# Router logits and token rows made from centred rows instead of normalised ones, in the last LayerNorm before the experts

## Chip, cores and metric

The kernel runs on one core of one Trainium2 chip. The metric is the device time of one execution in microseconds (us); the number quoted is the median of several executions.

## What is computed

One inference step of a two-layer trunk, for 304 tokens at once (16 learned meta tokens, 256 prompt tokens, 8 x 4 sample tokens), width 1024. Layer 0 is a convolution mixer and a dense SwiGLU, layer 1 is latent attention and an expert SwiGLU. The part that is changed is the norm after the attention, and what is made from its result:

```python
xp = layer_norm(ALPHA * xp + mp, ln_g[i, 0], ln_b[i, 0])        # (x - mu) * rsqrt(var + eps) * g + b
...
logits = jnp.einsum('btd,de->bte', x, w_router)                 # 8 experts
top_val, top_idx = lax.top_k(logits, 2)
...
out = out + gate[..., e:e + 1] * swiglu(x, w_gu[e], w_down[e], 3584)   # weights of 8 experts, fp32
```

Everything is fp32. A large product is made of three products of rounded ("fp32r") halves, `hi*hi + hi*lo + lo*hi`; small ones are plain fp32 products, which the profile shows as two passes of PE each.

## The kernel before

Work of each engine is written out by hand as one queue per engine, in program order, with counting semaphores between them; nothing is scheduled by a planner. Activations lie feature-major: `work` and `xres` are 128 partitions x 8 chunks x 304 tokens.

The stages around the change, in order:

- The attention's output product: four units of weights, `linear(U_MOUT + i, ...)` for i = 0 to 3 in `product_and_norm(3, ...)`. After each, DVE adds the residual (`residual`) into two chunks of `work`, and `norm_sums` prepares the sums for mean and variance. After unit 3, PE sums over partitions with a matrix of ones (`sum_up`, L2244) and then runs 18 products whose result nobody reads (`idle`, L2249).
- `layer_norm(3, xres, split_x=False)` on DVE: mean (L1547), its square (L1548), subtract the mean from chunk c (`center`, L1543), variance (L1553); ACT takes the root (L1080); DVE the reciprocal (L1557); then for each chunk a multiply by the reciprocal (L1561), with the centring of a later chunk between. ACT applies the norm's weight and bias to each chunk, `work` to `xres` (L1269).
- Router: PE multiplies `w_rt` (8 columns) with each chunk of `xres` (L2691, 8 products, 304 columns), DVE copies the 8 x 304 logits out of PSUM to `lgT` (L1909), PE turns them so that tokens lie on partitions (L2699), DVE copies that to `lg` (L1911, L1912).
- Token rows: PE turns `xres` into token rows, `for i in range(6)`, three token blocks (128, 128, 48) x two halves, four transposes each (L2702) into the PSUM banks `ROW_BANKS`. The turn of the logits stands after i = 0. ACT evicts every bank twice, to `xt_hi` (L1277) and `xt` (L1278).
- DVE ranks the logits (L1916 to L1930), PE counts the tokens of each expert (L2705, L2707) after its rows are turned, DVE ranks the experts by count (L1937 to L1947). Its result `first_i` raises the semaphore `ranked`.
- SP waits for `ranked` (L862), reads the four expert numbers, and only then issues the first of the 336 loads of expert weights, 1 MB each (L857). Before it no expert is known, so nothing of these weights is loaded.
- Meanwhile DVE works out the places of the rows (to L1974), PE runs 27 idle products, then gathers token rows by one-hot products (L2737, L2750), and the units of the expert stage begin (L2719 to L2726).

## Time and profile before

| | |
|---|---|
| median of 3 runs | 1714.94 us (1713.08 to 1717.51) |
| the profiled execution | 1709.49 us |
| its span, first to last instruction | 1707.8 us |
| PE busy | 1600.1 us (94%) |
| DVE busy | 998.8 us (58%) |
| ACT busy | 750.7 us (44%) |
| mean granted clock of TensorE | 0.971 |

The profiled execution has 1.7 us around its span, and is 5.4 us below the median of the runs. Times below are counted from the start of its span. PE is TensorE, PEld its weight loads, DVE VectorE, ACT ScalarE, POOL GpSimd, SP SyncE. A merged row of a timeline gives the start of the first instruction and the time to the end of the last. A matmul's own duration holds the time through the array; what counts in a stream of them is the distance from start to start.

### The profile page before, as it was taken

The page shows a single profiled execution, that of the slowest core. Times are in us where ns is not written, and L with a number is a line of the kernel's source. Part 1 is how long each engine was busy: PE and PEld are TensorE (multiplying, and loading weights), DVE is VectorE, ACT ScalarE, POOL GpSimd, SP SyncE. Part 2 cuts the span into 40 slices and gives each one's busy share as a digit, 9 for nine tenths or more (in the row PEclk, how much of TensorE's full clock was granted, in tenths as well). Part 3 has the DMA queues.
Part 4 walks back from the last instruction along what each step waited for, and adds up shares of the span by engine and source line. Part 5 has one row for each costly group of instructions (what it writes and reads, how often), then busy time and mean ns, then how long its engine had stood idle before and what let it go on. Part 6 is the DMA issues. An engine that isn't in the chain of part 4 may idle for free.

```text
span 1707.8 us, 27459 instructions
## 1 busy us (share of the span) xinstructions
PE 1600.1 (94%) x10674; PEld 1214.3 (71%) x10674; DVE 998.8 (58%) x1233; ACT 750.7 (44%) x829; POOL 139.0 (8%) x247
## 2 busy tenths in 40 slices
PE   8989999999998999999899989787899999999997
PEld 6768999998966666854444535454688888888775
DVE  4668655446645554572213312231788888888797
ACT  4215544235443223252213212221677777777675
POOL 1231000000032441020000000000000000000300
PEclk9999999999999999999999999887999999999999
DMA  9969555443241440059999999999999999999992
GB/s 234 257 156 304 147 161 153 136 139 129 67 140 48 127 142 27 2 203 409 404 397 404 406 405 399 404 403 384 410 407 361 398 371 376 399 371 369 394 392 100
DMA packets 232253, 466.83 MB, mean 273 GB/s; under 512 B 25206, under 2 KB 121621, under 8 KB 232130
## 3 DMA queue, kind: packets, MB, share of 16 engines
q1 hardware_dynamic: 217246, 426.81, 68.6%
q0 software_dynamic: 11744, 31.62, 6.1%
q10 hardware_dynamic: 3155, 6.93, 1.1%
q8 instruction: 72, 1.18, 0.3%
q14 instruction: 36, 0.29, 0.1%
HBM read 445.78 MB, written 19.99 MB: 273 GB/s over the span
## 4 chain that ended last, share of the span: by engine, by line
PE 77%; DMA 9%; DVE 7%; ACT 5%; issue 2%; SPq 0%; POOL 0%; ACTq 0%; DVEq 0%; POOLq 0%
PE ps L2726 10%; PE ps L2882 8%; PE ps L2884 7%; PE ps L2883 7%; PE ps L2163 7%; PE ps L2165 7%; PE ps L2164 7%; DMA raw<-in_moe_w_gu 5%; PE ps L2719 3%; DMA raw<-in_moe_w_down 3%; PE ps L2720 2%; PE ps L2721 2%; PE ps L2568 2%; PE ps L2531 2%; PE ps L2607 2%
## 5 line engine op out<-in xcount | busy, mean ns | idle before, releaser
L2014 DVE TENSOR_TENSOR w_lo<-raw,w_hi 128x2048 fp32r<-128x2048 f32 x168 | 383.3, 2291 | 63.9 <-ACT w_hi L1302 62.9
L1302 ACT ACTIVATE w_hi<-raw 128x2048 fp32r<-128x2048 f32 x168 | 322.3, 1919 | 130.2 <-PE ps L2884 110.1
L2020 DVE TENSOR_TENSOR w_lo<-raw,w_hi 128x2048 fp32r<-128x2048 f32 x42 | 96.3, 2292 | 229.8 <-ACT w_hi L1309 228.9
L2163 PE MATMUL ps<-x_hi,w_hi 128*128 128x304 f32 x656 | 202.7, 309 | 2.4 <-DVE x_lo L1566 1.8
L2165 PE MATMUL ps<-x_lo,w_hi 128*128 128x304 f32 x656 | 198.0, 302 | 0.0
L2164 PE MATMUL ps<-x_hi,w_lo 128*128 128x304 f32 x656 | 197.2, 301 | 0.0
L2882 PE MATMUL ps<-w_hi,g_hi 128*128 128x512 f32 x448 | 177.5, 396 | 9.2 <-DVE w_lo L2014 9.2
L2884 PE MATMUL ps<-w_hi,g_lo 128*128 128x512 f32 x448 | 175.6, 392 | 0.0
L1437 DVE TENSOR_TENSOR w_lo<-raw,w_hi 128x2048 fp32r<-128x2048 f32 (+4 forms) x129 | 135.5, 1099 | 68.3 <-ACT w_hi L1044 68.0
L2883 PE MATMUL ps<-w_lo,g_hi 128*128 128x512 f32 x448 | 175.3, 391 | 0.0
L2726 PE MATMUL ps<-raw,g_s 128*32 128x128 f32 (+3 forms) x1920 | 160.9, 377 | 8.7 <-DMA raw<-in_moe_w_gu 8.7
L1309 ACT ACTIVATE w_hi<-raw 128x2048 fp32r<-128x2048 f32 x42 | 80.3, 1912 | 160.6 <-DMA raw<-in_moe_w_gu 67.6
L1044 ACT ACTIVATE w_hi<-raw 128x2048 fp32r<-128x2048 f32 (+4 forms) x129 | 115.5, 950 | 78.9 <-PE ps L2165 58.9
L2726 PEld LDWEIGHTS ps<-raw,g_s 128*32 128x32 f32 (+1 forms) x1920 | 75.3, 120 | 91.9 <-issue 64.7
L2163 PEld LDWEIGHTS ps<-x_hi,w_hi 128*128 128x128 f32 x656 | 123.3, 188 | 9.5 <-DVE x_lo L1566 4.9
L2164 PEld LDWEIGHTS ps<-x_hi,w_lo 128*128 128x128 f32 x656 | 123.5, 188 | 0.5
L2165 PEld LDWEIGHTS ps<-x_lo,w_hi 128*128 128x128 f32 x656 | 123.3, 188 | 0.0
L2882 PEld LDWEIGHTS ps<-w_hi,g_hi 128*128 128x128 f32 x448 | 84.6, 189 | 29.5 <-DVE w_lo L2014 12.4
L2884 PEld LDWEIGHTS ps<-w_hi,g_lo 128*128 128x128 f32 x448 | 84.7, 189 | 18.0
L2883 PEld LDWEIGHTS ps<-w_lo,g_hi 128*128 128x128 f32 x448 | 84.9, 189 | 17.0
L2882 PE MATMUL ps<-w_hi,hT_hi 128*128 128x512 f32 x224 | 88.9, 397 | 0.6 <-DVE w_lo L2014 0.6
L2883 PE MATMUL ps<-w_lo,hT_hi 128*128 128x512 f32 x224 | 87.7, 392 | 0.0
(472 smaller groups left out, 2512.3 us busy)
## 6 DMA issues: line engine op xcount, KB each, us to landing
raw<-in_moe_w_gu SPq DMA_DIRECT2D x224, 1024.0 KB, 10.5
raw<-in_moe_w_down SPq DMA_DIRECT2D x112, 1024.0 KB, 10.0
raw<-in_ffn_w_gu SPq DMA_DIRECT2D x44, 512.0 KB, 5.2
raw<-in_conv_w_in SPq DMA_DIRECT2D x16, 512.0 KB, 7.7
raw<-in_ffn_w_down SPq DMA_DIRECT2D x16, 512.0 KB, 4.1
kvn<-in_cache_ckv POOLq DMA_DIRECT2D x64, 128.0 KB, 3.5
kvn<-in_cache_ckv SPq DMA_DIRECT2D x64, 128.0 KB, 2.8
rows_in<-zrow POOLq DMA_DIRECT2D x13, 512.0 KB, 10.3
```

Of the source, the lines that this page charges most:

```text
L1044: last = nc.scalar.activation(o, i, ACT.Copy)
L1302: nc.scalar.activation(w_hi[:, u % SPLIT], raw[:, u % RAW], ACT.Copy).then_inc(hi_done, 1)
L1437: last = V.tensor_tensor(lo, src, hi.bitcast(F32), ALU.subtract)
L2014: V.tensor_tensor(w_lo[:, u % SPLIT], raw[:, u % RAW], w_hi[:, u % SPLIT].bitcast(F32), ALU.subtract).then_inc(lo_done, 1)
L2020: V.tensor_tensor(w_lo[:, n % F_SPLIT], first_raw(k), w_hi[:, n % F_SPLIT].bitcast(F32), ALU.subtract).then_inc(lo_done, 1)
L2163: nc.tensor.matmul(out, hi, xh, start=start, stop=False, skip_group_check=True)
L2164: nc.tensor.matmul(out, lo, xh, start=False, stop=False, skip_group_check=True)
L2165: return nc.tensor.matmul(out, hi, xl, start=False, stop=stop, skip_group_check=True)
L2726: m = nc.tensor.matmul(ps[ROWS[x] * a:ROWS[x] * a + ROWS[x], bank, 0:n], rows, w[:, c0 + n * a:c0 + n * a + n], start=start, stop=stop, sk ...
L2882: nc.tensor.matmul(ps[:, bank, :], hi, wh, start=start, stop=False, skip_group_check=True)
L2883: nc.tensor.matmul(ps[:, bank, :], hi, wl, start=False, stop=False, skip_group_check=True)
L2884: m = nc.tensor.matmul(ps[:, bank, :], lo, wh, start=False, stop=stop, skip_group_check=True)
```

## The change

The normalised `xres` of this norm is no longer made. The router and the token rows are made of the centred `work`, before the multiplication by the reciprocal of the standard deviation:

- The norm's weight goes into the router's weights (`w_rt_g`, one DVE product) and into eight diagonal matrices (`gain`, eight ACT copies of the identity scaled by it). Turning a token row is then a real fp32 product with a diagonal matrix, not a transpose.
- The norm's bias goes in by products with one row of contraction: eight small products make the bias' share of the logits (`c_row`, made inside `mla_out(3)`), one product of `c_row` with the row of standard deviations adds it to the logits, and six (`row_bias`) put bias times standard deviation under the token rows, one for each bank of `ROW_BANKS`.
- The reciprocal is applied when PSUM is read: by DVE's multiplication that makes `lgT`, and as ACT's scale in the twelve evictions; three one-column products and two DVE copies turn it into `row_scale`.
- 14 of the 18 idle products are dropped.

```diff
+    w_rt_g = cmp2
+    c_row = ex[0:1, 11]
+    b_row = acc[0:1, 2]
+    last_rstd = sq[:, DC - 3]
+    gain = mo("gain", [P, DC, P])
+    row_scale = sq[:, DC - 4, 0:3]
...
         pool.wait_ge(x_split, DC * 4)
         pool.wait_ge(stores, 9 * 16)
         pool.dma_start(w_rt[:], moe_w_router[0].rearrange("(c p) e -> p c e", p=P)).then_inc(rt_w, 16)
+        pool.dma_start(b_row, ln_b[1, 0:1]).then_inc(rt_w, 16)
...
-        pool.wait_ge(ln_scaled, DC * 4)
+        pool.wait_ge(ln_centred, centred(3, DC - 1))
...
 
+        act.wait_ge(unit_used, U_MOUT + 1)
+        for c in range(DC):
+            nc.scalar.activation(gain[:, c], ident[:], ACT.Copy, scale=lng[:, 2, c:c + 1])
+        act.wait_ge(rt_pe, 1)
+        nc.scalar.activation(c_row, ps[0:1, 7, 0:NEXP], ACT.Copy).then_inc(rt_act, 1)
+
         squares(3, range(DC - 2))
         root(3)
-        for c in range(DC):
-            act.wait_ge(ln_scaled, DC * 3 + c + 1)
-            nc.scalar.activation(xres[:, c], work[:, c], ACT.Identity, scale=lng[:, 2, c:c + 1], bias=lnb[:, 2, c:c + 1]
-                                 ).then_inc(ln_hi, 1)
 
         act.wait_ge(stores, 9 * 16)
+        act.wait_ge(rt_dve, 1)
         for i in range(6):
             b, hf = divmod(i, 2)
             n = TB[b][1]
             act.wait_ge(rt_pe, ROWS_TURNED[i])
-            nc.scalar.activation(xt_hi[0:n, b, 512 * hf:512 * hf + 512], ps[0:n, ROW_BANKS[i], :], ACT.Copy)
-            nc.scalar.activation(xt[0:n, b, 512 * hf:512 * hf + 512], ps[0:n, ROW_BANKS[i], :], ACT.Copy).then_inc(rt_act, 1)
-        act.wait_ge(rt_dve, 1)
+            nc.scalar.activation(xt_hi[0:n, b, 512 * hf:512 * hf + 512], ps[0:n, ROW_BANKS[i], :], ACT.Copy, scale=row_scale[0:n, b:b + 1])
+            nc.scalar.activation(xt[0:n, b, 512 * hf:512 * hf + 512], ps[0:n, ROW_BANKS[i], :], ACT.Copy, scale=row_scale[0:n, b:b + 1]
+                                 ).then_inc(rt_act, 1)
+        act.wait_ge(rt_dve, 2)
         nc.scalar.activation(tk[:, 3], tk[:, 2], ACT.Exp).then_inc(rt_act, 1)
 
...
                     V.tensor_tensor(x_lo[:, c - 1], out[:, c - 1], x_hi[:, c - 1].bitcast(F32), ALU.subtract).then_inc(x_split, 1)
+
+        def centre(n, between):
+
+            mean_at, var_at = ln_banks[n]
+            v.wait_ge(ln_mean, 2 * n + 2)
+            chain(V.tensor_scalar(ln_delta, ps[:, mean_at, 0:T], 1.0 / D, None, ALU.mult))
+            mark(V.tensor_tensor(ln_dsq, ln_delta, ln_delta, ALU.mult))
+            squared = n_own[0]
+            for c in range(DC):
+                V.tensor_tensor(work[:, c], work[:, c], ln_delta, ALU.subtract).then_inc(ln_centred, 1)
+                if c == 0:
+                    v.wait_ge(dve, squared)
+                    v.wait_ge(ln_var, n + 1)
+                    V.scalar_tensor_tensor(out=rstd[:], in0=ps[:, var_at, 0:T], scalar=1.0 / D, in1=ln_dsq,
+                                           op0=ALU.mult, op1=ALU.subtract).then_inc(ln_ready, 1)
+                if c >= 2:
+                    between(c - 2)
+            between(DC - 2)
+            between(DC - 1)
+            v.wait_ge(ln_std, n + 1)
 
...
             split(U_MOUT + i + AHEAD)
+            if i == 3:
+                v.wait_ge(rt_w, 32)
+                V.tensor_tensor(w_rt_g[:], w_rt[:], lng[:, 2].unsqueeze(2).broadcast_to([P, DC, NEXP]), ALU.mult)
             residual(U_MOUT + i, G_MOUT + i, 2 * i)
             norm_sums(3, i)
         distance(3, (DC - 2, DC - 1))
-        layer_norm(3, xres, split_x=False)
+        centre(3, lambda c: None)
+        chain(V.reciprocal(last_rstd, rstd[:]))
 
         def acc_start(b):
...
 
         v.wait_ge(rt_const, 9 + FIRST_JOBS)
-        v.wait_ge(rt_pe, 1)
-        V.tensor_copy(lgT, ps[0:NEXP, 2, 0:T]).then_inc(rt_logits, 1)
-        v.wait_ge(rt_pe, 3)
+        v.wait_ge(rt_pe, 2)
+        V.tensor_tensor(lgT, ps[0:NEXP, 2, 0:T], last_rstd[0:NEXP], ALU.mult).then_inc(rt_logits, 1)
+        v.wait_ge(rt_pe, 4)
+        V.tensor_copy(row_scale[:, 0:2], ps[:, 4, ROW_SCALE:ROW_SCALE + 2])
+        V.tensor_copy(row_scale[0:TAIL, 2:3], ps[0:TAIL, 4, ROW_SCALE + 2:ROW_SCALE + 3]).then_inc(rt_dve, 1)
         mark(V.tensor_copy(lg[:, 0:2], ps[:, 4, 0:2 * NEXP].rearrange("p (b e) -> p b e", e=NEXP)))
         chain(V.tensor_copy(lg[0:TAIL, 2], ps[0:TAIL, 4, 2 * NEXP:3 * NEXP]))
...
                     sum_up(mean_at, rstd[:], True, True).then_inc(ln_mean, 1)
+            if n == 3:
+                pe.wait_ge(rt_act, 1)
             pe.wait_ge(ln_ready, ln_base(n) + 3)
             pe.wait_ge(ln_sq, DC * n + DC - 2)
             shift_and_spread(n, [(var_at, sq[:, 0], True), (mean_at, rstd[:], True),
                                  (var_at, sq[:, 4], False), (var_at, sq[:, 5], False)])
-            idle(22 if n < 3 else 18, 0)
+            idle(22 if n < 3 else 4, 0)
 
         pe.wait_ge(ln_cent, DC - 2)
...
         pe.wait_ge(x_split, 4 * DC)
-        product_and_norm(3, G_MOUT, lambda i: linear(U_MOUT + i, G_MOUT + i, 8, blocks, *X))
-
-        pe.wait_ge(rt_w, 16)
+
+        def mla_out(i):
+
+            if i == 3:
+                pe.wait_ge(rt_w, 32)
+                for c in range(DC):
+                    m = nc.tensor.matmul(ps[0:1, 7, 0:NEXP], lnb[:, 2, c:c + 1], w_rt[:, c], start=c == 0, stop=c == DC - 1,
+                                         skip_group_check=True)
+                m.then_inc(rt_pe, 1)
+            linear(U_MOUT + i, G_MOUT + i, 8, blocks, *X)
+
+        product_and_norm(3, G_MOUT, mla_out)
+
+        def row_bias(i):
+
+            b, hf = divmod(i, 2)
+            t0, n = TB[b]
+            nc.tensor.matmul(ps[0:n, ROW_BANKS[i], :], rstd[0:1, t0:t0 + n], b_row[:, 512 * hf:512 * hf + 512], start=True, stop=False,
+                             skip_group_check=True)
+
         pe.wait_ge(group_free, G_MOUT + 4)
         for c in range(DC):
-            pe.wait_ge(ln_hi, DC * 4 + c + 1)
-            m = nc.tensor.matmul(ps[0:NEXP, 2, 0:T], w_rt[:, c], xres[:, c], start=c == 0, stop=c == DC - 1)
+            if c == 5:
+                pe.wait_ge(ln_std, 4)
+                nc.tensor.matmul(ps[0:NEXP, 2, 0:T], c_row, rstd[0:1], start=False, stop=False, skip_group_check=True)
+                row_bias(0)
+            pe.wait_ge(ln_centred, centred(3, c))
+            m = nc.tensor.matmul(ps[0:NEXP, 2, 0:T], w_rt_g[:, c], work[:, c], start=c == 0, stop=c == DC - 1, skip_group_check=True)
         m.then_inc(rt_pe, 1)
+        for i in range(1, 6):
+            row_bias(i)
         for i in range(6):
             b, hf = divmod(i, 2)
             t0, n = TB[b]
             if i == 1:
                 pe.wait_ge(rt_logits, 1)
                 for a, (t1, w) in enumerate(TB):
-                    m = nc.tensor.transpose(ps[0:w, 4, NEXP * a:NEXP * a + NEXP], lgT[:, t1:t1 + w], ident[0:NEXP, 0:NEXP])
+                    nc.tensor.transpose(ps[0:w, 4, NEXP * a:NEXP * a + NEXP], lgT[:, t1:t1 + w], ident[0:NEXP, 0:NEXP])
+                    m = nc.tensor.matmul(ps[0:w, 4, ROW_SCALE + a:ROW_SCALE + a + 1], last_rstd[:, t1:t1 + w], ident[:, 0:1],
+                                         start=True, stop=True, skip_group_check=True)
                 m.then_inc(rt_pe, 1)
             for c in range(4):
-                m = nc.tensor.transpose(ps[0:n, ROW_BANKS[i], P * c:P * c + P], xres[:, 4 * hf + c, t0:t0 + n], ident[:])
+                m = nc.tensor.matmul(ps[0:n, ROW_BANKS[i], P * c:P * c + P], work[:, 4 * hf + c, t0:t0 + n], gain[:, 4 * hf + c],
+                                     start=False, stop=c == 3, skip_group_check=True)
             m.then_inc(rt_pe, 1)
-        pe.wait_ge(rt_dve, 1)
+        pe.wait_ge(rt_dve, 2)
         nc.tensor.matmul(ps[:, 4, 0:3 * NEXP], before[:], selt[:].rearrange("p b e -> p (b e)"), start=True, stop=False, skip_group_check=True)
         for a in range(3):
```

`centred(3, c)` is c + 1. Other semaphore targets move by one with the new signals (`rt_act`, `rt_dve`, `rt_pe`). The rest of the kernel is as before.

PE's queue at the last unit of the output product. The names are lines of each kernel's own file: L2163 to L2165 before are L2216 to L2218 now (the three fp32r products), L2244 is L2297 (`sum_up`), L2746 is new. Before:

```order
L2164 MATMUL ps<-x_hi,w_lo 128x304
L2165 MATMUL ps<-x_lo,w_hi 128x304
L2244 MATMUL ps<-rstd,ones 128x304
L2163 MATMUL ps<-x_hi,w_hi 128x304
L2164 MATMUL ps<-x_hi,w_lo 128x304
```

Now:

```order
L2217 MATMUL ps<-x_hi,w_lo 128x304
L2218 MATMUL ps<-x_lo,w_hi 128x304
L2297 MATMUL ps<-rstd,ones 128x304
L2746 MATMUL ps<-w_rt,vec 1x8 x8
L2216 MATMUL ps<-x_hi,w_hi 128x304
L2217 MATMUL ps<-x_hi,w_lo 128x304
```

Eight products of one column of weights and eight moving columns stand between unit 2 and unit 3.

PE's queue from the sums of the norm to the count. Before (L2691 router, L2702 token rows, L2699 the logits' turn, L2705 and L2707 the count):

```order
L2249 MATMUL ps<-idle_w 128x512 x18
L2691 MATMUL ps<-xres,w_rt 8x304 x8
L2702 MATMUL ps<-ident,xres 128x128 x4
L2699 MATMUL ps<-ident,sg 128x8 x2
L2699 MATMUL ps<-ident,sg 48x8
L2702 MATMUL ps<-ident,xres 128x128 x12
L2702 MATMUL ps<-ident,xres 48x128 x8
L2705 MATMUL ps<-selt,before 128x24
L2707 MATMUL ps<-selt,ones 128x24
L2707 MATMUL ps<-selt,ones 128x16
```

Now, from the idle products on (L2767 router, L2764 the logits' bias, L2757 `row_bias`, L2782 token rows, L2777 the logits' turn, L2778 the reciprocal's turn):

```order
L2302 MATMUL ps<-idle_w 128x512 x4
L2767 MATMUL ps<-work,cmp_153 8x304 x5
L2764 MATMUL ps<-rstd,ex 8x304
L2757 MATMUL ps<-acc,rstd 128x512
L2767 MATMUL ps<-work,cmp_153 8x304 x3
L2757 MATMUL ps<-acc,rstd 128x512 x3
L2757 MATMUL ps<-acc,rstd 48x512 x2
L2782 MATMUL ps<-gain,work 128x128 x4
L2777 MATMUL ps<-ident,sg 128x8
L2778 MATMUL ps<-ident,sq 128x1
L2777 MATMUL ps<-ident,sg 128x8
L2778 MATMUL ps<-ident,sq 128x1
```

Then follow one more pair of L2777 and L2778 for the last 48 tokens, the other twenty L2782 and the count. Between the router's last product and the logits' turn there stood four transposes; now there stand five one-row products of 512 columns and four real products.

DVE's queue from the centring to the ranking. Before the multiplications (L1561) and centrings (L1543) alternate after the reciprocal (L1557):

```order
L1543 TENSOR_TENSOR work<-work,ln_rows 128x304
L1553 SCALAR_TENSOR_TENSOR rstd<-ps,ln_rows 128x304
L1543 TENSOR_TENSOR work<-work,ln_rows 128x304
L1557 RECIPROCAL rstd<-rstd 128x304
L1561 TENSOR_TENSOR work<-work,rstd 128x304
L1543 TENSOR_TENSOR work<-work,ln_rows 128x304
L1561 TENSOR_TENSOR work<-work,rstd 128x304
```

Now (L1603 centring, L1607 variance, L1942 reciprocal, L1960 `lgT`, L1962 and L1963 `row_scale`, L1964 `lg`):

```order
L1603 TENSOR_TENSOR work<-work,ln_rows 128x304
L1607 SCALAR_TENSOR_TENSOR rstd<-ps,ln_rows 128x304
L1603 TENSOR_TENSOR work<-work,ln_rows 128x304 x7
L1942 RECIPROCAL sq<-rstd 128x304
L1960 TENSOR_TENSOR sg<-ps,sq 8x304
L1962 COPY sq<-ps 128x2
L1963 COPY sq<-ps 48x1
L1964 COPY lg<-ps 128x16
```

All eight chunks are centred before the reciprocal, and the eight multiplications are gone.

## Rows read from the trace of the kernel before

**Rows 1.** Busy by window: PE, PEld, DVE, ACT, POOL; then clock, DMA share, GB/s.
```profile
736.70:740.10 3.40, 1.82 (x17) 1.50 (x15) 3.09 (x14) 3.40 (x9) 0.00 (x0) 1.00 0.00 0
740.20:743.60 3.40, 3.40 (x11) 2.72 (x11) 2.93 (x22) 2.35 (x4) 0.00 (x0) 0.50 0.00 0
...
746.00:750.00 4.00, 4.00 (x19) 2.99 (x18) 3.86 (x9) 0.00 (x0) 2.46 (x2) 1.00 0.91 323
...
1100.00:1200.00 100.00, 80.09 (x931) 51.91 (x923) 23.66 (x18) 20.52 (x22) 1.99 (x4) 0.85 1.02 396
...
1300.00:1400.00 100.00, 99.97 (x455) 82.49 (x454) 87.88 (x44) 75.29 (x46) 0.00 (x0) 1.00 1.00 378
```

**Rows 2.** What SP's DMA queue waited for (us, times, longest), and its timeline.
```profile
SPq L862 <- DVE first_i L1947: 99.1, 1, 99.1
...
744.83 15.70 SPq L857 DMA_DIRECT2D raw<-in_moe_w_gu  x8
```

**Rows 3.** Timeline of PE, 719 to 757 (start, us, engine, line).
```profile
722.82 1.19 PE L2244 MATMUL ps<-sq,ones 128*128 128x304 f32 x4
723.61 4.51 PE L2249 MATMUL ps<-idle_w 128*128 128x512 f32 x18
...
734.45 0.66 PE L2702 MATMUL ps<-ident,xres 128*128 128x128 f32 x4
735.14 0.31 PE L2699 MATMUL ps<-ident,sg 8*128 8x8 f32 x3
735.38 2.40 PE L2702 MATMUL ps<-ident,xres 128*128 128x128 f32 x20
739.37 0.40 PE L2705 MATMUL ps<-selt,before 128*128 128x24 f32 x2 [1.58 <-DVE tk L1930]
```

**Rows 4.** Timeline of DVE, 712 to 768.
```profile
719.95 0.85 DVE L1591 SCALAR_TENSOR_TENSOR work<-xres,ps 128x304 f32<-128x304 f32 x2 [1.60 <-PE ps L2165]
...
723.92 0.47 DVE L1543 TENSOR_TENSOR work<-work,ln_rows 128x304 f32<-128x304 f32 x1
...
725.39 2.05 DVE L1557 RECIPROCAL rstd<-rstd 128x304 f32<-128x304 f32 x1 [0.23 <-ACT rstd L1080]
...
734.62 0.46 DVE L1909 COPY sg<-ps 8x304 f32<-8x304 f32 x1 [1.66 <-PE ps L2691]
735.49 0.17 DVE L1911 COPY lg<-ps 128x16 f32<-128x16 f32 x1 [0.40 <-PE ps L2699]
...
740.57 0.17 DVE L1937 SCALAR_TENSOR_TENSOR ex<-ps,eidx 128x8 f32<-128x8 f32 x1
...
742.26 0.17 DVE L1947 CAST first_i<-first_f 128x4 int32<-128x4 f32 x1
```

**Rows 5.** Chain that ended last, 722 to 747.
```profile
733.30 1.21 PE ps L2691 x4
```

**Rows 6.** Timeline of PE, five other places.
```profile
26.62 0.68 PE L2214 MATMUL ps<-ident,tap_rows 31*128 31x31 f32 x8
...
486.56 7.13 PE L2441 MATMUL ps<-wuv,ckvT 128*128 128x512 f32 x16
...
524.60 0.85 PE L2480 MATMUL ps<-ckvT,kt 128*128 128x272 f32 x3
525.38 0.72 PE L2481 MATMUL ps<-krT,kt 32*128 32x272 f32 x2
526.03 0.95 PE L2480 MATMUL ps<-ckvT,kt 128*128 128x272 f32 x3
...
536.07 0.61 PE L2515 MATMUL ps<-pT,ckvN 128*128 128x128 f32 x4
```

**Rows 7.** Timeline of ACT, 695 to 770.
```profile
714.66 2.39 ACT L1074 ACTIVATE sq<-work 128x304 f32<-128x304 f32 x6 [13.29 <-DVE work L1492]
...
735.20 0.60 ACT L1277 ACTIVATE xt_hi<-ps 128x512 fp32r<-128x512 f32 x1 [1.41 <-PE ps L2702]
...
740.46 0.61 ACT L1278 ACTIVATE xt<-ps 48x512 f32<-48x512 f32 x1
```

More of the change, by code:

```diff
@@ L453, in ln_base, with centred, scaled, xres_count @@
         return 0 if n == 0 else DC + 2 + 4 * (n - 1)
+    DEFERRED = (3,)
+    def centred(n, c):
+        return DC * DEFERRED.index(n) + c + 1
+    def scaled(n, c):
+        return DC * n + c + 1
+    def xres_count(n):
+        return DC * len([q for q in DEFERRED if q <= n])
     def group_bank(g):
@@ L489, in build @@
     ln_scaled = sem("ln_scaled")
+    ln_centred = sem("ln_centred")
     ln_hi = sem("ln_hi")
@@ L656, in build @@
     ROW_BANKS = (7, 0, 1, 3, 5, 6)
-    ROWS_TURNED = (2, 4, 5, 6, 7, 8)
-    COUNTED = 9
+    ROWS_TURNED = (3, 5, 6, 7, 8, 9)
+    COUNTED = 10
+    ROW_SCALE = 4 * NEXP
     PAIRS = HEADS // 2
@@ L987, in _ @@
         nc.gpsimd.memset(valid[0:TAIL, 2], 1.0).then_inc(rt_const, 1)
-        pool.wait_ge(rt_act, 6)
+        pool.wait_ge(rt_act, 7)
         pool.wait_ge(y_st, 16)
@@ L1990, in weights @@
         def weights():
-            v.wait_ge(rt_act, 7)
+            v.wait_ge(rt_act, 8)
             chain(V.tensor_scalar(tk[:, 4], tk[:, 3], 1.0, None, ALU.add))
@@ L2757, in gather @@
             gather_lower(c)
-        pe.wait_ge(rt_act, 1)
+        pe.wait_ge(rt_act, 2)
         idle(27, ROW_BANKS[0])
-        pe.wait_ge(rt_act, 6)
+        pe.wait_ge(rt_act, 7)
         for c in range(3):
```

6 lines of the change are left out of this document (3 added, 3 removed).

## The prediction

> **What bounds the kernel now.** I read the busy time by window first, for the stage in which the weights of the experts come. Between 736.7 and 743.6 DMA moves nothing [rows 1]; from 746 on it is busy without a gap, still at 396 GB/s and a share of 1.02 in 1100:1200, where PE is busy for only 80 of 100 us. By 1300:1400 PE is busy 99.97 of 100. So the weights are the bound up to about 1200 and PE after it, and PE's stage starts when the weights' stage is over. Nothing between them gives time back: whatever moves the first load moves the end by as much. Then I read what SP waits for. Its queue waits once for `first_i`, 99.1 us, and issues the first of the expert loads at 744.83 [rows 2]. `first_i` is made by L1947 at 742.26 [rows 4]; the 2.6 us between are SP reading four numbers. The question is thus only when L1947 runs. The reader should not look at PE's 94% here, nor at the gather that follows: the chain that the profile prints runs through the idle products, but the DMA queue is what is full.
>
> Now backwards from L1947. It stands 1.7 us behind L1937 (740.57), which waits for the count; the count begins on PE at 739.37, after PE sat idle for 1.58 us, waiting for DVE's L1930 [rows 3, 4]. That ranking starts with the copy of `lg` at 735.49, and that follows the logits' turn (735.14), which follows `lgT` (734.62), which follows the router's last product. The chain shows that product's last four passes from 733.30 [rows 5]; ahead of it are the multiplications on DVE, fed by the reciprocal (725.39, 2.05 us) and spaced so that one chunk comes every two DVE instructions, about 0.77 us (two such in a row take 0.85, 0.38 more than one). So before the change DVE sets the pace from 723 to 740, and PE waits.
>
> **Prices.** Each from a row, as distance from start to start.
> - fp32 pass over 304 columns: the last four of the router take 1.15 us to L2702's start at 734.45 [rows 3, 5]; without 0.09 for a change of shape that is 0.265, a product 0.53.
> - 512 columns: 16 passes in 7.13; less 0.1 for the first load and 0.16 for the last one's way through the array 0.43 a pass, 0.84 ns a column, a product 0.86 [rows 6].
> - 128 columns, 128 rows of contraction, new weights for each: four passes in 0.61; less the same 0.16 0.11 a pass, a product 0.22 [rows 6].
> - Changing how many rows of the array are used: two passes of 32 rows and 272 columns run from 525.38 to 526.03, 0.65; at 0.84 ns a column they would take 0.46 [rows 6]. A change costs 0.19 with its first load, which is then not hidden; 0.1 when the new weights are a few columns.
> - Tiny passes: eight in 0.68, less 0.16 0.065 each [rows 6].
> - Nothing in the trace contracts over one row. The 32-row pass is nearest and streams like any other, so a one-row product of 512 columns is taken at 0.86. From below it could cost no more than a tiny product, 0.13; from above, 0.86 plus an unhidden load of 0.1 for each pass, 1.06.
>
> **The change, step by step**, on the clock of the profiled span.
> 1. The bias' share of the logits, ahead of unit 3 (PE streams without a gap there, so it is all on the path): 16 tiny passes at 0.06 and two changes, 0.3: **+1.2** (from 0.7, if a pass costs half of that, to 2.1 at the 0.11 of a full load). ACT's eight `gain` copies fall into its 13.29 idle ahead of 714.66 [rows 7]. Its `c_row` copy delays the squares by under 1 us; they end 2.4 us after 714.66, and PE needs them at 720. The 64-column `w_rt_g` fits into DVE's 1.60 idle [rows 4]. The extra 4 KB load by POOL is 20 us early. All times below are without this 1.2.
> 2. PE's sums end at 723.84 [rows 3]. Four idles at 0.23 (18 in 4.51): 724.8. Five router products at 0.53, whose chunks are centred one every 0.39 from 723.92 on and so are there in time: 727.5.
> 3. `c_row`'s product 0.6, `row_bias(0)` 0.19 + 0.86, change back and three router products 0.1 + 1.6: 730.9. That is **3.5 earlier** than before (734.4). DVE's reciprocal starts after the eighth centring at 727.4 and is done at 729.5, so it is hidden. `lgT` can be read 0.27 later, and is done at 731.6. POOL's `iota` is released at 727.5 and is no wait.
> 4. But PE is in order, and the turn of the logits stands behind the other biases: 0.19 + 5 x 0.86 + 0.13 = 4.6, to 735.5; then the four products of i = 0, 0.2 + 8 x 0.11 = 1.1, to 736.6.
> 5. The turn is now three pairs, each an 8-row transpose and a 128-row product of one column; each pair changes rows twice. 2 x 0.52 + 0.36 for the 48-token one, and 0.1 to get in: 1.5, to 738.1, where before three transposes took 0.31 [rows 3].
> 6. DVE reads 0.15 later and first makes two copies of `row_scale` (0.18): `lg` at 738.4, against 735.49: **+2.9**. L1930 is later by the same.
> 7. The count stands behind twenty real products, 40 passes at 0.11 with a change to 48 columns: 4.6, to 742.7 + 0.1. Before, twenty transposes took 2.40 and ended well before L1930. L1930 gives its signal at 739.3 + 2.9 = 742.2, so PE is now the later one: the count starts at 742.8 against 739.37, **+3.4**. The last of it no longer falls into the stretch at clock 0.50 [rows 1], -0.1.
> 8. ACT's evictions wait for `row_scale` and start at 738.5. Twelve at the pace of before (735.20 to 740.46 for eleven, 0.48 [rows 7]) are over by 744.3; the first four, which DVE's `xt_lo` of the first block needs, at 740.6. DVE comes there at 742.2 and has 1.7 us until it can read the count (which took 1.2 from 739.37 to 740.57 [rows 3, 4]); it did this subtraction in that same gap before. Hidden; if it were not, at most 1 us.
> 9. ACT's eight `xres` copies and DVE's eight multiplications are gone, but they were the path up to 733 only, which step 3 has counted.
>
> Sum: 1.2 + 3.4 - 0.1 = **+4.5 us** at L1937, at SP's first load and at the end. Against the profiled execution 1709.49 + 4.5 = 1714.0; against the median of the runs shown, which is 5.4 higher, 1714.94 + 4.5 = **1719.4 us**, 0.26% slower. A measurement of this kernel tells about 0.3%, or 5.1 us, from no change, so I expect "the same" a little more often than "slower".
>
> The gather moves by less: PE's 27 idle products took 7.9 us because the clock was 0.50 for 3.4 of them [rows 1] and will take 6.2. The weights do not wait for it.
>
> A rule against the change: 40 passes at 0.11 suppose that the next 128 columns of weights load under the running pass, as the four passes of [rows 6] show. The Trainium skill ("TensorE: Matmul & The Clock Gate", Measured speedup vs the span model) says that loads overlap running products only when they use other rows of the array. By that rule each of the 48 passes would pay a load of its own as well; the trace disagrees, 0.11 for load and pass together. Worked out from the rows, 48 more loads at 0.11 would be +5.3, and 1724.7; that is a rival below.
>
> **Rivals.**
> - A clock that falls (slower). PE's clock was 1.2 GHz from 740.2 to 743.6, after a stretch in which PE had been busy 1.82 of 3.40 us [rows 1]. Five products that use one row of 128 may count as little work; the records would show PE busy. For it: 4.6 us of them in a row. Against: before, the clock held through streams of narrow work and fell behind a stretch with idle time, and now PE has none from 713 to 750. Price: 3.4 us at half the clock lose 1.7, twice that loses 3.4: +6.2 to +7.9, so 1721 to 1723. It decides from 0.6 us lost.
> - Loads not hidden under the real products, as above: 1724.7.
> - One-row products as cheap as tiny ones: steps 3 and 4 shrink by 0.7 and 3.7, the turn ends at 733.7, the count starts at 738.4, -1.0 + 1.2 = about 0: 1715. Against it: no row shows columns that stream faster for fewer rows.
> - The lateness is absorbed, for example because loads were waiting for free places and not for DMA: 1715. Against it: the share of DMA is over 1 all along.
>
> **Chances.** Forecast 0.64, of it a quarter beyond 5.1 us, since the tiny passes and the six changes of rows may each be off by half a microsecond and two executions differ by 2. Clock 0.16, unhidden loads 0.04, cheap one-row products 0.09, absorbed 0.07. Slower by over 0.3%: 0.16 + 0.14 + 0.04 = 0.34. Faster by over 0.3%: 0.03, where a cheap case meets a lucky clock later. Same: 0.63. Range: below, the cheap cases at 1715 less 1; above, the clock's 1723: 1714 to 1723. The forecast's own range is 1717.5 to 1721.
>
> **What would show it.** The first expert load at about 749.4 instead of 744.83, and `lg` copied at 739.7 (735.49). `row_bias` 1 to 5 at 0.86 each and in one piece, between the router's end (about 732) and the first L2782. L2777 and L2778 spread over 1.5 us. PE reaching the count after L1930's signal. A clock of 1.00 from 720 to 750. The prediction is wrong if the first load comes before 746 or after 751, if the one-row products take well under 0.8 each, or if the end does not follow the first load.

## The result and the profile after

| | before | changed |
|---|---|---|
| median | 1716.13 us, 10 runs (1711.14 to 1721.43) | 1719.55 us, 10 runs (1716.93 to 1728.3) |
| profiled execution | 1709.49 us, span 1707.8 | 1718.25 us, span 1716.6 |
| mean granted clock | 0.971 | 0.974 |

The ratio is 1.0034, 95% interval 1.0017 to 1.005: slower by 5.8 us (2.9 to 8.6); the two medians alone are 3.4 apart. A second set of executions, in the experiments below, gave 1.006 (1.0037 to 1.0082).

First the windows, as [rows 1], here for PE alone (time, busy, count; clock; DMA's share; GB/s).

```profile
727.00:735.50 8.50, 8.50 (x26) 1.00 0.00 0
735.50:745.70 10.20, 10.20 (x36) 0.50 0.00 0
...
800.00:900.00 100.00, 93.05 (x586) 0.97 1.03 403
```

The stage of the weights is as before: DMA full (1.03), and by 1300:1400 PE full (99.97 of 100 us). New is the second row. For 10.2 us TensorE's granted clock is 0.50, its lower level of 1.2 GHz, although PE is busy for every one of them. Before, this place had a stretch of 3.4 us at 0.50, after one in which PE had been partly idle [rows 1].

SP's timeline, as [rows 2], with the first expert load:

```profile
754.09 11.96 SPq L879 DMA_DIRECT2D raw<-in_moe_w_gu  x7
```

The first load comes 9.26 us later than in [rows 2], and the span is 8.8 longer: the end follows the load. PE's timeline, as [rows 3], shows where the time goes. L2297 are the sums, L2767 the router, L2757 `row_bias`, L2782 the `gain` products, L2777 and L2778 the turn of logits and reciprocals, L2786 the count.

```profile
725.24 0.42 PE L2297 MATMUL ps<-sq,ones 128*128 128x304 f32 x1
...
726.51 2.73 PE L2767 MATMUL ps<-work,cmp 128*8 128x304 f32 x10
...
729.77 1.12 PE L2757 MATMUL ps<-acc,rstd 1*128 1x512 f32 x2
...
732.46 6.15 PE L2757 MATMUL ps<-acc,rstd 1*128 1x512 f32 x10
738.54 2.08 PE L2782 MATMUL ps<-gain,work 128*128 128x128 f32 x8
740.54 0.27 PE L2777 MATMUL ps<-ident,sg 8*128 8x8 f32 x1
...
742.36 6.43 PE L2782 MATMUL ps<-gain,work 128*128 128x128 f32 x40
748.72 0.40 PE L2786 MATMUL ps<-selt,before 128*128 128x24 f32 x2
```

The ten one-row passes in a row take 6.15 us; over full rows at full clock ten such passes will take 4.69 in fullrow2 below. The clock falls three microseconds after the first of them, and the eight passes behind them (2.08; in fullrow2 1.16), the turn, and the first 3.3 us of the last forty run at the lower level. The count starts at 748.72; before it was 739.37 [rows 3].

DVE, as [rows 4]: `lgT`, `lg`, the last instruction of the ranking, the wait for the count.

```profile
732.66 0.46 DVE L1960 TENSOR_TENSOR sg<-ps,sq 8x304 f32<-8x304 f32 x1 [1.58 <-PE ps L2767]
...
742.61 0.15 DVE L1964 COPY lg<-ps 128x16 f32<-128x16 f32 x1
...
746.26 0.16 DVE L1983 TENSOR_TENSOR tk<-tk 128x3 f32<-128x3 f32 x1
...
749.82 0.17 DVE L1990 SCALAR_TENSOR_TENSOR ex<-ps,eidx 128x8 f32<-128x8 f32 x1 [2.26 <-PE ps L2788]
```

The roles have turned round. In [rows 3] PE waited 1.58 us for the ranking; now the ranking is done at 746.4, and DVE waits 2.26 us for PE's count. `lgT` is early (732.66; before 734.62 in [rows 4]), `lg` 7.1 late: the gain of the router is made, and is then lost in PE's queue.

**Reading the distance.** Two executions differ before the changed place is reached, so I count from the last pass of the sums (it starts 0.42 before the end of its row): 725.24 here, 723.58 before. Of these 1.66, step 1 is 0.68: from the sums' two passes behind unit 2 to the second product of unit 3 it is 1.33 here and 0.65 before (712.56 to 713.21).

```profile
713.53 0.68 PE L2297 MATMUL ps<-rstd,ones 128*128 128x304 f32 x2
714.14 0.55 PE L2746 MATMUL ps<-w_rt,vec 128*1 128x8 f32 x16
...
714.86 0.30 PE L2217 MATMUL ps<-x_hi,w_lo 128*128 128x304 f32 x1
```

From the sums to the first load it is 28.85 us, before 21.25: +7.60. So the change costs 0.68 + 7.60 = 8.3 in this trace; the other 1.0 is a difference between executions, and 0.5 is won behind the load.

### The profile page after: what moved, and what is told of

Its sections match the earlier page's. It is cut to its first block, busy times and chain, and to the rows that moved or that the text cites. A ratio compares the mean times of both kernels' runs of the same rounds, so it can differ in the third digit from the quotient of the medians.

```text
span 1716.6 us, 27547 instructions
## 1 busy us (share of the span) xinstructions
PE 1605.2 (94%) x10720; PEld 1216.8 (71%) x10720; DVE 996.2 (58%) x1228; ACT 749.6 (44%) x830; POOL 142.0 (8%) x248
## 4 chain that ended last, share of the span: by engine, by line
PE 75%; DMA 10%; DVE 5%; ACT 5%; issue 4%; POOL 0%; ACTq 0%; SPq 0%; DVEq 0%; POOLq 0%
PE ps L2807 10%; PE ps L2963 8%; PE ps L2964 8%; PE ps L2965 8%; PE ps L2216 7%; DMA raw<-in_moe_w_gu 7%; PE ps L2218 6%; PE ps L2217 6%; PE ps L2800 2%; PE ps L2801 2%; PE ps L2802 2%; DMA raw<-in_moe_w_down 2%; PE ps L2623 2%; PE ps L2586 2%; PE ps L2662 2%
## 5 line engine op out<-in xcount | busy, mean ns | idle before, releaser
L2216 PE MATMUL ps<-x_hi,w_hi 128*128 128x304 f32 x656 | 203.0, 309 | 2.7 <-DVE x_lo L1593 1.7
L2218 PE MATMUL ps<-x_lo,w_hi 128*128 128x304 f32 x656 | 198.3, 302 | 0.0
L2807 PE MATMUL ps<-raw,g_s 128*32 128x128 f32 (+3 forms) x1920 | 162.5, 381 | 10.2 <-DMA raw<-in_moe_w_gu 10.2
L2216 PEld LDWEIGHTS ps<-x_hi,w_hi 128*128 128x128 f32 x656 | 123.4, 188 | 10.1 <-DVE x_lo L1593 4.9
L2218 PEld LDWEIGHTS ps<-x_lo,w_hi 128*128 128x128 f32 x656 | 123.5, 188 | 0.0
```

The source lines that it names most:

```text
L2216: nc.tensor.matmul(out, hi, xh, start=start, stop=False, skip_group_check=True)
L2218: return nc.tensor.matmul(out, hi, xl, start=False, stop=stop, skip_group_check=True)
L2807: m = nc.tensor.matmul(ps[ROWS[x] * a:ROWS[x] * a + ROWS[x], bank, 0:n], rows, w[:, c0 + n * a:c0 + n * a + n], start=start, stop=stop, sk ...
```

## The experiments

My theory: PE's queue is what is late, by 3 to 4 us through its order (biases and twenty products ahead of turn and count) and by 4 to 5 through the clock, which falls because the bias products contract over one row. Rivals: the clock falls for another reason (14 fill products fewer, the waits of the turn); the ranking and not PE's queue sets the end; the end does not hang on this place.

All runs in one table. The columns are the sums' last pass, from it to the first expert load, from the load to the end of the span (us, profiled execution), then the medians timed, in runs beside the kernel before.

| kernel | sums | to load | to end | span | median | ratio (95%) |
|---|---|---|---|---|---|---|
| before | 723.58 | 21.25 | 963.0 | 1707.8 | 1715.2 to 1716.1 | 1 |
| changed | 725.24 | 28.85 | 962.5 | 1716.6 | 1719.55 | 1.0034 (1.0017 to 1.005) |
| after2 | 726.87 | 28.85 | 967.8 | 1723.5 | 1725.07 | 1.006 (1.0037 to 1.0082) |
| fullrow | 729.86 | 24.27 | 966.0 | 1720.1 | 1719.36 | 1.0027 (1.0003 to 1.0051) |
| fullrow2 | 727.91 | 24.28 | 964.1 | 1716.3 | 1719.94 | 1.003 (1.0011 to 1.0049) |
| turnfirst | 729.83 | 27.36 | 967.1 | 1724.3 | 1720.46 | 1.0029 (1.001 to 1.0047) |
| nobias | 725.35 | 18.60 | 962.2 | 1706.2 | 1712.39 | 0.9994 (0.9972 to 1.0017) |
| idle18 | 727.54 | 32.02 | 962.0 | 1721.6 | 1723.79 | 1.005 (1.0028 to 1.0073) |
| best | 726.30 | 16.96 | 968.9 | 1712.2 | 1715.27 | 1.0 (0.9984 to 1.0016) |
| best1 | 730.43 | 16.95 | 975.4 | 1722.8 | 1722.08 | 1.004 (1.002 to 1.006) |
| best2 | 727.71 | 16.96 | 962.4 | 1707.1 | 1712.99 | 0.9989 (0.9971 to 1.0006) |
| b_row1 | 729.38 | 28.61 | 962.4 | 1720.4 | 1722.05, one run | |
| b_row32 | 729.44 | 25.22 | 965.7 | 1720.4 | 1722.09, one run | |
| b_row128 | 732.62 | 21.68 | 966.2 | 1720.5 | 1722.29, one run | |

The second column repeats to 0.01 us in the two kernels that were profiled twice (changed and after2, fullrow and fullrow2), while the sums move by up to 9 between all these executions, and the single times with them. It is the column to read. nobias leaves the norm's bias out of the token rows; it is there for its time alone.

### Full bias rows (fullrow, fullrow2)

```diff
-    b_row = acc[0:1, 2]
+    b_row = acc[:, 2]
...
-        pool.dma_start(b_row, ln_b[1, 0:1]).then_inc(rt_w, 16)
+        pool.dma_start(b_row, ln_b[1, 0:1].broadcast_to([P, D])).then_inc(rt_w, 16)
...
+        nc.scalar.activation(b_row, b_row, ACT.Copy, scale=1.0 / P)
...
-            nc.tensor.matmul(ps[0:n, ROW_BANKS[i], :], rstd[0:1, t0:t0 + n], b_row[...], start=True, stop=False,
+            nc.tensor.matmul(ps[0:n, ROW_BANKS[i], :], rstd[:, t0:t0 + n], b_row[...], start=True, stop=False,
```

> The changed kernel, with the bias row held in all 128 partitions (scaled by 1/128 on ScalarE) and the bias products contracting over 128 rows, as many as the other products have, instead of over one; same number of products, same order. Theory A, that the products which contract over one row let TensorE's clock fall (the changed kernel showed 0.5 for 10.24 us from 735.52): no stretch at half clock between 720 and 760, the bias' passes 0.43 us each throughout, the twenty products .11 us a pass, the first expert load (SP's L879) 24 to 25.5 us behind the last pass of norm 3's sums instead of 28.85, the time 1714 to 1717. Theory B, that the clock fell for another reason, such as TensorE's shorter fill products or its waits for the turn of the logits: the stretch stays where it was, and with it 28.5 to 29 us and 1718 to 1722.

> The changed kernel with 128-row bias products once more, beside the unchanged one on the same chip. Theory A (the full rows save the 4 to 5 us of half clock in each execution): 3 to 5 us below the changed kernel, ratio to the kernel before 1.0005 to 1.0025. Theory B (the half clock costs less in time than in the stretch, because the transfers behind it absorb part, or the wider copy of the bias row costs elsewhere): within 2 us of the changed kernel.

PE's timeline of fullrow2 (L2759 the biases, L2784 the `gain` products):

```profile
735.13 4.69 PE L2759 MATMUL ps<-acc,rstd 128*128 128x512 f32 x10
739.75 1.16 PE L2784 MATMUL ps<-gain,work 128*128 128x128 f32 x8
740.84 0.22 PE L2779 MATMUL ps<-ident,sg 8*128 8x8 f32 x1
...
742.07 4.82 PE L2784 MATMUL ps<-gain,work 128*128 128x128 f32 x40
746.82 0.40 PE L2788 MATMUL ps<-selt,before 128*128 128x24 f32 x2
```

Its window:

```profile
720.00:763.90 43.90, 42.48 (x217) 1.00 0.24 84
```

And SP's first load:

```profile
752.19 15.29 SPq L879 DMA_DIRECT2D raw<-in_moe_w_gu  x8
```

Same instructions, same order, as many of them, and the clock holds at 1.00 past the first load. The half clock is gone with the one-row contraction, and with it 4.57 us from sums to load (28.85 to 24.28, both twice). The time of a pass itself does not hang on the rows: at full clock `row_bias(0)` takes 1.05 us to the next product's start with 1 row (729.77 to 730.82) and 1.06 with 128.

The plain executions show it less clearly. Timed side by side the full rows are 5.1 us faster (1719.94, 12 runs, against 1725.07, 6 runs), but fullrow's 1719.36 is only 0.2 below the first set of the changed kernel (1719.55), and the intervals of the ratios overlap. That the half clock costs 4.57 us up to the load is shown; how much of it reaches the median is not settled. My times of 1714 to 1717 were too low: I had taken 4 us off the changed kernel's median, not off the 8.3 that its trace costs. The ratios of fullrow2 (1.003) and after2 (1.006) lie above what I expected as well.

### The changed kernel again (after2)

> The changed kernel once more, unchanged, for a second profile and more executions. Theory A (the half clock comes in every execution, since the one-row products run in each): a stretch of 6.8 us or more at .50 begins within 4 us of the third bias product again, first load 27 to 30 us behind the sums; ratio 1.003 to 1.005. Theory B (the profiled execution happened on it): no such stretch, first load 24.3 us behind.

Two windows of after2:

```profile
737.40:747.50 10.10, 10.10 (x38) 0.51 0.00 0
764.70:771.40 6.70, 6.68 (x44) 0.51 1.04 415
```

The stretch is there again and again 10 us long, within the bias products, and the distance to the load is 28.85 to the hundredth. It belongs to the kernel. The second row is another stretch, at the gather and the first expert's products, which the first profile had not, and one more follows from 778 to 785: the load-to-end column is 5.3 larger here. So in this kernel such late stretches come and go with the execution. fullrow has one of nearly 7 us from 762, fullrow2 one of 3.4 from 764, turnfirst two. fullrow and fullrow2 have no one-row bias, so these late stretches do not need one.

### Without the bias, and with more fill (nobias, idle18)

```diff
-                row_bias(0)
...
-        for i in range(1, 6):
-            row_bias(i)
```

> The changed kernel without its twelve two-pass bias products; the token rows lack the norm's bias. Theory A (one-row products cost the queue time, and the clock falls with them): about 5.2 us of products gone at full clock, 4 to 5 us of half clock gone as well, so the first load 19 to 20.5 us behind the sums' last pass instead of 28.85 (the kernel before: 21.25), clock 1.00 through 720 to 750, time 1710 to 1713. Theory B (the clock falls because of the shorter fill or the waits in this stretch, whatever the bias does): a stretch at half clock stays near 735, first load 22 to 25 us behind the sums.

```diff
-            idle(22 if n < 3 else 4, 0)
+            idle(22 if n < 3 else 18, 0)
```

> The changed kernel with 18 fill products behind norm 3's sums, as the kernel before has, instead of 4. Theory A (the one-row products let the clock fall): the stretch at half clock stays, begun within the bias products again, and the 14 further fill products, 4 us, delay the router by what VectorE has not yet to do, 2 to 3.2 us: first load 30 to 32.5 us behind the sums' last pass, time 1720 to 1724. Theory B (it was the shorter fill): no half clock, first load 26 to 28.5 us behind the sums, time 1717 to 1719.

A window of nobias:

```profile
720.00:800.00 80.00, 77.51 (x490) 1.00 0.70 273
```

And one of idle18, of its stretch:

```profile
741.30:751.50 10.20, 10.20 (x39) 0.50 0.00 0
```

nobias takes out six products, that is twelve passes; the bias' share of the logits stays. Without the six the clock holds, through the same short fill and the same turn, and the load comes 18.60 behind the sums, a little earlier than I had expected. With 18 fill products it falls, for the same 10.2 us. So the fill is not the cause. Its removal is the part of the change that pays: 32.02 against 28.85, 3.2 us. And nobias is 2.65 quicker from sums to load than the kernel before: that is what the centred rows and the shorter fill are worth together, without the bias of the token rows (2.0 after step 1).

### The turn ahead of the biases (turnfirst)

```diff
         for i in range(1, 6):
             row_bias(i)
-        for i in range(6):
-            b, hf = divmod(i, 2)
-            t0, n = TB[b]
             if i == 1:
                 pe.wait_ge(rt_logits, 1)
...
                 m.then_inc(rt_pe, 1)
+        for i in range(6):
+            b, hf = divmod(i, 2)
+            t0, n = TB[b]
             for c in range(4):
```

On PE's queue the turn now stands behind `row_bias(1)`, not ahead of all the biases as the expectation has it; `row_bias` 2 to 5 and all 24 products follow it.

> The changed kernel, with the turn of the logits and the reciprocals ahead of the bias products 0 to 5 on TensorE's queue instead of behind them. Theory A, that the order on TensorE makes the ranking late: lg (L1964) comes 3 to 6 us earlier against the sums' last pass than in the changed kernel, but the count then waits for the bias and the twenty products behind the turn, which come to 4.6 + 2.4 us at full clock: the first load moves by 0 to -2 us only, time 1717 to 1720, the half clock still there. Theory B, that the ranking on VectorE sets the end and not TensorE's queue: the first load follows lg, 3 to 6 us earlier, time 1713 to 1716.

PE's timeline of turnfirst:

```profile
739.18 4.75 PE L2757 MATMUL ps<-acc,rstd 1*128 1x512 f32 x8
743.86 8.04 PE L2782 MATMUL ps<-gain,work 128*128 128x128 f32 x48
751.83 0.40 PE L2786 MATMUL ps<-selt,before 128*128 128x24 f32 x2
```

DVE's, with `lg` and the wait for the count:

```profile
739.43 0.16 DVE L1964 COPY lg<-ps 128x16 f32<-128x16 f32 x1
752.93 0.17 DVE L1990 SCALAR_TENSOR_TENSOR ex<-ps,eidx 128x8 f32<-128x8 f32 x1 [2.72 <-PE ps L2788]
```

And its window at the lower clock:

```profile
742.10:748.80 6.70, 6.70 (x26) 0.50 0.00 0
```

`lg` comes 9.6 us behind the sums instead of 17.4, more than I expected, and the load only 1.5 earlier. The ranking is not what is late; the count waits for PE's queue. Even the 1.5 need not come from the order: the half clock lasts 6.7 us here and not 10.2, and by my estimate 3.5 us less at half speed are 1.7 us of work won back.

### The same fall in the kernel before (b_row1, b_row32, b_row128)

```diff
-            idle(22 if n < 3 else 18, 0)
+            if n < 3:
+                idle(22, 0)
+            else:
+                for _ in range(8):
+                    nc.tensor.matmul(ps[:, 0, :], ones[0:1], ones[0:1].unsqueeze(1).broadcast_to([1, 4, P]), start=True, stop=True,
+                                     skip_group_check=True)
```

(`ones[0:32]` and `ones[0:128]` in the other two.)

> The kernel before; its 18 fill products behind norm 3's sums (128 rows, 512 columns) are replaced by 8 four-byte products of 512 columns that contract over one row, 16 passes of about .43 us. Theory A (products over one row let the clock fall): a half-clock stretch of 3.4 us or more begins between 724 and 735, where the kernel before has 1.00, and passes of .85 us show in it. Theory B (they do not; the changed kernel's fall had other causes): 1.00 from 715 to 738, all passes .43 us. The time says little: the fill ends within 1 us of where it did at full clock, 3 to 4 us later at half.

> As the last one, with the 8 products contracting over all 128 rows. Theory A: 1.00 from 715 to 738, passes .43 us. Theory B (any swap of the fill does it): the same stretch as with one row.

> The kernel before with 8 four-byte products of 512 columns over 32 rows in place of the 18 fill products (1 row: a half-clock stretch of 13.65 us from 732.01, within the products, 28.6 us from the sums to the first load; 128 rows: none until 763, and 21.7). If what matters grows with the rows of the array that work, 32 of 128 should still let the clock fall: a stretch begins 2 to 6 us behind the sums' last pass. If only very few rows do it: 1.00 until 760, 21.7 us.

The sixteen passes on PE's timeline, with 1 row:

```profile
729.74 11.79 PE L2337 MATMUL ps<-ones 1*128 1x512 f32 x16
```

Its window:

```profile
732.10:745.60 13.50, 13.50 (x21) 0.50 0.00 0
```

With 32 rows:

```profile
729.79 8.43 PE L2337 MATMUL ps<-ones 32*128 32x512 f32 x16
```

Its window:

```profile
735.70:742.40 6.70, 6.70 (x12) 0.51 0.00 0
```

With 128 rows:

```profile
732.87 7.03 PE L2337 MATMUL ps<-ones 128*128 128x512 f32 x16
```

Its window:

```profile
720.00:760.00 40.00, 37.64 (x184) 1.00 0.12 39
```

One number is changed between the three, how many rows the products contract over, and PE is busy throughout the products and the stretches. With 1 row the clock is 0.50 for 13.5 us, with 32 for 6.7 (from 6.3 us behind the sums, a little later than I expected), with 128 it does not fall here; from sums to load it is 28.6, 25.2 and 21.7 us. Each is one execution. This shows the cause without anything else of the change. It is not the only cause of a fall: b_row128 has a late stretch too, with PE just as busy, and so has b_row32.

```profile
763.00:769.40 6.40, 6.40 (x43) 4.17 (x43) 5.04 (x11) 2.30 (x3) 3.37 (x3) 0.50 1.04 415
```

The single times of the three say nothing here, since the sums of the last came 3.2 us later than those of the others.

### Another order on PE (best, best1, best2)

PE's queue in best: router, products 0, the three transposes of the logits alone, the three reciprocals (into bank 2, copied in the middle of the ranking), products 1 to 3, the count, then the rest, with each bias last in its bank. DVE's `xt_lo` of the first block moves behind the picks, the one-hot matrices that gather the token rows.

```diff
+        row_products(0)
+        pe.wait_ge(rt_logits, 1)
+        for a, (t1, w) in enumerate(TB):
+            m = nc.tensor.transpose(ps[0:w, 4, NEXP * a:NEXP * a + NEXP], lgT[:, t1:t1 + w], ident[0:NEXP, 0:NEXP])
+        m.then_inc(rt_pe, 1)
...
+        for i in range(1, 4):
+            row_products(i)
         pe.wait_ge(rt_dve, 2)
...
+        for i in range(6):
+            if i >= 4:
+                row_products(i)
+            row_bias(i)
```

best has full bias rows, best1 the one-row ones.

> Full output. TensorE's queue in another order: router, products of rows 0, the logits' three transposes alone (a signal of their own), the three reciprocals (in bank 2, copied to the scales in the middle of the ranking), products of rows 1 to 3, the count, then products 4 and 5 and the six bias products, each last in its bank; the bias contracts over 128 rows. Theory A, that the changed kernel lost its gain only by what stands ahead of the turn and the count on TensorE: lg 8.0 to 8.5 us behind the sums' last pass (17.37 in the changed kernel, 11.91 before), TensorE waits for the ranking instead of the other way round, the first expert load 17.3 to 18.3 us behind the sums (21.25 before, 28.85 changed), the clock 1.00 throughout, time 2 to 3.5 us below the kernel before, 1712 to 1714. Theory B, that what is deferred comes back behind the load (evictions and gather late, products of the first expert late): first load as in A, but the time within 1 us of the kernel before.

> The same order, the bias contracting over one row as in the changed kernel. The six one-row products, ten passes of them back to back, now run behind the count, where the first load no longer waits for them. Theory A (few-row products let the clock fall wherever they stand in a row of ten or so): a half-clock stretch begins within them, at 24 to 30 us behind... the count, that is 740 to 750 on the span, but the first load is at 17.3 to 18.3 us behind the sums as with full rows, and the time is within 1.5 us of that kernel's. Theory B (the clock fell in the changed kernel because of where they stood, before the tiny products of the turn): no half clock between 720 and 760.

PE's timeline of best:

```profile
737.90 0.40 PE L2791 MATMUL ps<-selt,before 128*128 128x24 f32 x2 [0.45 <-DVE tk L1986]
...
746.02 6.44 PE L2305 MATMUL ps<-idle_w 128*128 128x512 f32 x27
752.30 0.31 PE L2827 MATMUL ps<-picks,xt_hi 128*128 128x320 f32 x1
...
761.53 1.93 PE L2816 MATMUL ps<-raw,g_s 128*32 128x128 f32 x32
```

ACT's last eviction:

```profile
746.72 0.67 ACT L1306 ACTIVATE xt<-ps,sq 48x512 f32<-48x512 f32 x1
```

SP's first load, and the ninth:

```profile
743.26 12.40 SPq L879 DMA_DIRECT2D raw<-in_moe_w_gu  x8
766.81 0.37 SPq L879 DMA_DIRECT2D raw<-in_moe_w_down  x1
```

And two windows:

```profile
757.10:763.90 6.80, 6.80 (x43) 0.50 1.03 419
764.00:800.00 36.00, 35.02 (x245) 1.00 0.87 328
```

PE waits for the ranking again, and the first load is 16.96 behind the sums, 4.3 us less than before the change: theory A to the load. But the time is that of the kernel before: theory B. The deferred products end at 746.02, then come the 27 fill products that once filled a wait. The rows are evicted at 747.4 and the picks ready then, but PE starts the gather (L2827) at 752.30, behind its fill. With a stretch at half clock in the gather on top, the first expert's products start 18.3 us behind the first load; before the change it was 10.8. The places of the loads come free late: the ninth load is issued 23.6 us behind the first (15.9 before the change), and DMA's share from 764 to 800 is 0.87.

In best1 the same order with one-row biases has its stretch behind the count (744.2 to 761.2), the load is as early, and the kernel is 6.8 us slower than best. I had expected at most 1.5. The fall slows the deferred products, which end 6.4 us later behind the sums than in best, and with them the fill and the gather: the first expert's products start 25.0 us behind the load instead of 18.3, and from load to end it is 6.5 more. Its window:

```profile
744.20:761.20 17.00, 17.00 (x37) 0.50 0.77 278
```

best2 tests the reading of best. Against best, the fill is cut from 27 to 4 and bias 0 stands ahead of the count, with products 3 behind it:

```diff
-        for i in range(1, 4):
-            row_products(i)
+        row_products(1)
+        row_products(2)
+        row_bias(0)
...
-        for i in range(6):
-            if i >= 4:
+        for i in range(1, 6):
+            if i >= 3:
                 row_products(i)
...
-        idle(27, ROW_BANKS[0])
+        idle(4, ROW_BANKS[0])
```

> The reordered kernel with full bias rows, with two more edits: the 27 fill products ahead of the gather, which ran from 746.02 to 752.3 there while the picks and the evicted rows were ready by 747.4, are cut to 4; and bias product 0 stands ahead of the count (products 3 behind it), so that the evictions begin earlier. Theory A (the 4.3 us won at the first load were given back because TensorE reached the first expert's products late, 18.3 us behind the first load instead of 10.8, and the loads stood still for want of freed buffers): first load again 17 to 18 us behind the sums' last pass, the gather 4 to 5 us earlier than there, the transfers' share from 746 to 800 back at 1.00 or more, time 2 to 3.5 us below the kernel before (ratio .998 to .9988). Theory B (the end does not hang on this stretch): ratio 1.0 again.

PE's timeline of best2:

```profile
747.47 1.20 PE L2305 MATMUL ps<-idle_w 128*128 128x512 f32 x4
748.89 0.42 PE L2828 MATMUL ps<-picks,xt_hi 128*128 128x320 f32 x1 [0.22 <-ACT xt L1306]
...
756.43 1.14 PE L2817 MATMUL ps<-raw,g_s 128*32 128x128 f32 x32
```

And its window:

```profile
764.00:800.00 36.00, 35.02 (x259) 1.00 1.03 412
```

The first expert's products start 11.8 us behind the load, the share is 1.03, and load to end is 962.4 again, 6.5 less than in best. Timed it is 3.0 us below the kernel before, ratio 0.9989. The interval reaches 1.0006, so that it beats the kernel before is likely and not shown; that it beats the changed kernel is (their intervals do not meet). The two traces also divide the 6.5. The gather starts 4.2 us behind the load here and 9.0 in best: 4.8 for the fill, since in best its inputs were there at 747.4, 4.1 behind the load, and the earlier bias brought nothing up to there. From the gather's start to the first expert's products it is 7.5 here and 9.2 in best: 1.7 for the stretch at half clock.

## Why the prediction was right, and where it was not

The forecast was 1719.4 us and the median 1719.55. The agreement is in part luck. The change costs 8.3 us in the trace where the forecast has 4.5; by medians the first set shows only 3.4, on a base that came out 1.2 above the one that I added to (1716.13 against 1714.94), and a second set of the same kernel gave 1725.07, above the range. The prediction's own sign of being wrong, a first load after 751, did come: 754.09, and 753.1 without the 1.0 between the executions. Two things happened together, my forecast and the rival to which I had given 0.16.

- **What bounds.** Right. From load to end it is 963.0 before and 962.5 after; in six of the table's fourteen rows it lies between 962.0 and 963.0, with no half clock between the load and 800; in the other eight (964.1 and more) some half clock falls on that stretch, on the gather or the first expert's products. best and best1 show a limit of the rule: where PE comes to the first expert 18 or 25 us behind the load, and not 11 or 12, the end follows PE.
- **Step 1**, +1.2. Mis-sized: 0.68. Sixteen tiny passes take 0.55 us with the 0.17 of the last one's own duration, so 0.025 from start to start, not 0.06. The Trainium skill ("TensorE: Matmul & The Clock Gate", Wait — 56ns, not 53.3ns?) gives about 25 ns as the least from start to start, and this row agrees.
- **Steps 2 and 3**, router over at 730.9 on the old clock. fullrow2, whose sums are 4.33 later than before, starts its next bias at 735.13, so 730.8: right.
- **Step 4**, 4.6 and 1.1. At full clock 4.62 (735.13 to 739.75) and 1.09: right, and so is the choice of 0.86 for a one-row product against the cheap end (1.05 and 1.06 for one and 128 rows, above). In the changed kernel they took 6.08 and 2.00, for the clock.
- **Step 5**, 1.5. 1.23 at full clock, 1.82 in the changed kernel.
- **Steps 6 and 7**, `lg` +2.9 and count +3.4. On the old clock fullrow2 has 737.99 (+2.5) and 742.49 (+3.1); PE came to the count 0.7 after the ranking, forecast 0.6. The forty passes took 4.75, so 0.12 each, loads hidden: that rival is out. (In the Trainium skill the rule on loads stands in "TensorE: Matmul & The Clock Gate" under The mechanism, and not under the heading that the prediction names; these passes do not follow it.)
- **Step 8**, evictions. Hidden, as said, but 0.57 each and not 0.48: reading the scale from a tile costs 0.09 (rows of the changed kernel, at full clock for PE again). "ScalarE: Activation LUTs" in the Trainium skill (What ACT_TABLE_LOAD costs) gives about 93 ns for such an operand; the rows agree.

```profile
747.21 0.69 ACT L1303 ACTIVATE xt_hi<-ps,sq 128x512 fp32r<-128x512 f32 x1
747.78 0.70 ACT L1304 ACTIVATE xt<-ps,sq 128x512 f32<-128x512 f32 x1
```

- **The sum**, +4.5. At full clock 0.68 + 3.03 = 3.7, mis-sized by the tiny passes and the turn. The kernel that the sum describes is the one with full rows, and it is at 1719.36 and 1719.94.
- **The clock**, the step that failed: "The last of it no longer falls into the stretch at clock 0.50", and a full clock for everything before. The fall was a rival at 1.7 or 3.4 us, held unlikely because "the clock held through streams of narrow work". The narrow work of [rows 6] had 32 rows for 0.65 us; it said nothing on 5 us of one row. In place of -0.1 there came 10.2 us at half clock from 735.5 on, in both profiles of the changed kernel, and they cost 4.57 up to the load, more than either price of the rival. Trace and table make the change 8.3 us slower, inside both timed intervals (2.9 to 8.6, and 6.3 to 14.1).

The Trainium skill, in "TensorE: Matmul & The Clock Gate" (What's actually happening), says that the clock follows how busy PE has been. By the busy time of the profile the windows above differ: busy 13.50 of 13.50 us and a clock of 0.50, and no fall with 128 rows.

Still open: why turnfirst's ten passes, broken by the turn, bring 6.7 us of half clock and not 10.2; and what puts the stretches between 757 and 787 into some executions, with PE busy.

## What to carry to other kernels

A product that contracts over one row takes TensorE as long as one over 128, and ten passes of such products in a row lowered the clock for what stood behind them. Where a bias is added by a product, spread it over all rows (scaled by 1/128) or keep such products very few; the two passes of `c_row`'s product, alone in nobias, did nothing. When a change takes work off the engine that sets the pace, look at what stands ahead of the hand-over in the other engine's queue: here 3.5 us were won at the router and 6.5 lost to what stands in front of the turn and the count, at full clock. And when work is moved behind the hand-over, take out the fill that stood there: in best it held the gather back by 4.8 us, and the gain was given back.

## What the runs showed of the hardware that I had not expected

- Granted clock and rows: 16 fp32 passes of 512 columns, PE busy throughout, gave 13.5 us at 0.50 with 1 row, 6.7 with 32, and no fall at their place with 128.
- Executions differ by up to 9 us before the changed place (sums at 723.58 before and at 732.62 in b_row128, whose code is the same up to there). In the first 130 us the granted clock is 1.00 in the one and 0.92 in the other, but that does not tell all: fullrow2 has 1.00 there as well, and its sums come at 727.91, 3.65 later than before the change even without step 1.
